# Rotary embedding of q and k without rotation products: 32-row blocks exchanged by ScalarE's copies

## What is computed

```
x1, x2 = xf[..., :half], xf[..., half:]
return jnp.concatenate([x1 * c - x2 * s, x2 * c + x1 * s], axis=-1)
```

## Time and profile before

| | |
|---|---|
| median of 3 runs | 912.7 us (911.99 to 912.81) |
| the profiled execution's own time | 912.49 us |
| its span, first to last instruction | 910.7 us |
| TensorE matmuls busy | 890.3 us, 98% |
| VectorE busy | 604.7 us, 66% |
| ScalarE busy | 454.3 us, 50% |
| GpSimd busy | 44.3 us, 5% |
| granted TensorE clock, mean | 0.998 |

### The profile page before, as it was taken

The page is one execution under the profiler, slowest core; times in us unless marked ns, Lnnn a source line. Parts: engine busy times, 40 slices in busy tenths (PEclk is TensorE's granted clock), DMA queues, the critical chain, the costliest instruction groups (busy, mean ns, idle before and its releaser), DMA issues.

```text
span 910.7 us, 15439 instructions
## 1 busy us (share of the span) xinstructions
PE 890.3 (98%) x6574; PEld 752.5 (83%) x6574; DVE 604.7 (66%) x966; ACT 454.3 (50%) x731; POOL 44.3 (5%) x61
## 2 busy tenths in 40 slices
PE   7999999999899999999999999999999999999997
PEld 5999988787789888888889978776788788888885
DVE  4577978557766666656766477877863566666673
ACT  4775444346443444546544356484622545555561
POOL 0010000010000000000000440000000000000000
PEclk9999999999999999999999999999999999999999
DMA  9544333233578665555339574353817566665521
GB/s 341 186 139 140 97 100 110 72 95 117 206 254 278 185 185 187 189 202 203 108 130 222 137 223 145 127 186 96 276 44 208 141 188 189 192 192 192 200 95 47
DMA packets 131205, 150.78 MB, mean 166 GB/s; under 512 B 11808, under 2 KB 102176, under 8 KB 131008
## 3 DMA queue, kind: packets, MB, share of 16 engines
q1 hardware_dynamic: 129920, 145.57, 51.6%
q10 hardware_dynamic: 1216, 4.23, 1.2%
HBM read 148.73 MB, written 1.05 MB: 164 GB/s over the span
## 4 chain that ended last, share of the span: by engine, by line
PE 90%; DVE 4%; ACT 2%; issue 2%; DMA 1%; POOL 0%; POOLq 0%; ACTq 0%; DVEq 0%
PE psum L834 12%; PE psum L721 10%; PE psum L723 9%; PE psum L722 9%; PE psum L839 7%; PE psum L807 4%; PE psum L808 4%; PE psum L816 4%; PE psum L787 4%; PE psum L727 3%; PE psum L883 2%; PE psum L893 2%; PE psum L884 2%; PE psum L840 2%; PE psum L1724 2%
## 5 line engine op out<-in xcount | busy, mean ns | idle before, releaser
L1827 ACT ACTIVATE parts<-low 128x1024 fp32r<-128x1024 f32 (+3 forms) x252 | 254.3, 1044 | 66.3 <-PE psum L723 50.2
L2710 DVE TENSOR_TENSOR parts<-low,parts 128x1024 fp32r<-128x1024 f32 (+3 forms) x156 | 187.9, 1234 | 27.6 <-ACT parts L1827 27.4
L721 PE MATMUL psum<-parts 128*128 128x512 f32 (+2 forms) x424 | 169.4, 399 | 1.8 <-DVE parts L2710 1.0
L723 PE MATMUL psum<-parts 128*128 128x512 f32 (+2 forms) x424 | 163.5, 386 | 0.0
L722 PE MATMUL psum<-parts 128*128 128x512 f32 (+2 forms) x424 | 163.4, 385 | 0.0
L1827 ACT ACTIVATE high<-psum 128x512 f32<-128x512 f32 (+4 forms) x95 | 52.4, 562 | 162.0 <-PE psum L840 76.4
L834 PE MATMUL psum<-parts 128*128 128x512 f32 x462 | 116.8, 392 | 0.0
L834 PEld LDWEIGHTS psum<-parts 128*128 128x128 f32 x462 | 86.9, 188 | 16.9
L721 PEld LDWEIGHTS psum<-parts 128*128 128x128 f32 x424 | 79.6, 188 | 23.3 <-issue 4.0
L723 PEld LDWEIGHTS psum<-parts 128*128 128x128 f32 x424 | 79.6, 188 | 16.3
L722 PEld LDWEIGHTS psum<-parts 128*128 128x128 f32 x424 | 79.8, 188 | 14.2 <-issue 0.2
(11 more groups left out here) (317 smaller groups left out, 1340.0 us busy)
## 6 DMA issues: line engine op xcount, KB each, us to landing
low<-in_w_in_dram SPq DMA_DIRECT2D x40, 1024.0 KB, 5.3
low<-in_w_ffn_in_dram SPq DMA_DIRECT2D x44, 512.0 KB, 5.2
low<-in_w_ff_in_dram SPq DMA_DIRECT2D x16, 1024.0 KB, 5.9
low<-in_w_ff_out_dram SPq DMA_DIRECT2D x16, 1024.0 KB, 4.9
low<-in_w_ffn_out_dram SPq DMA_DIRECT2D x11, 1024.0 KB, 4.9
low<-in_w_out_dram SPq DMA_DIRECT2D x8, 1024.0 KB, 5.3
low<-in_w_ple_gate_dram SPq DMA_DIRECT2D x4, 1024.0 KB, 4.9
low<-consts_dram ACTq DMA_DIRECT2D x1, 2142.0 KB, 9.0
```

Of the source, the lines that this page charges most:

```text
L721: mm(o, l[0], r[0], start, False)
L723: return mm(o, l[1], r[0], False, stop)
L1827: return e.activation(o, a, ACT.Copy)
L2710: tt(rslot3(n, nk, width)[:, r, 0:w], slot3(n, nk, width)[:, r, 0:w], st.hi3(j)[:, r, 0:w].bitcast(F32), ALU.subtract) \
```

## The change

- The constant rotation matrix goes, and with it `rotate` of TensorE and its 11 products. The table of constants is 128 columns shorter. The table of sines now holds -sin in the first 32 rows of each head and +sin in the other 32.
- ScalarE's `rope_read` makes four copies of 32 rows out of the bank (`swapped`), each to the neighbouring 32-row block, and signals behind the fourth. In block two they go straight to the place of the result (`rope_to`), so the buffers `rz2` go.
- VectorE's sine product takes the exchanged copy in SBUF instead of the product in PSUM, and in block two works in place.
- In block two VectorE makes the cosine product too, from the chunk's bank, at the start of its turn for the next chunk and before the sine product. The bank is freed by this product and no longer by ScalarE's copy. GpSimd keeps the sum. VectorE waits for GpSimd's sum of chunk n - 2 before it writes `rt2` again.
- In block one the cosine product still comes from VectorE, in its old place, and waits as before for ScalarE's signal, which now stands behind the fourth copy.

```diff
-            def rotate(tag, n, m, z):
-
-                b = 2 + n % 2 if tag == "qk" else 5 + n % 3
-                p = bank(b)
-                q.wait_ge(*rope_act.at(tag, n))
-                mm(p[:, 0:256 * m], const(C_ROT, 128), z, True, True).then_inc(rope_pe.up(tag, n), 1)
-                free[b] = [rope_dve.at(tag, n)]
...
             def read2(n):
-                return [main_act.at("qa", n) if n < 2 else rope_act.at("in2", n)]
+                return [main_act.at("qa", n) if n < 2 else rope_dve.at("in2", n, "cos")]
...
+            def swapped(dst, z):
+
+                for p in range(4):
+                    t = copy(dst[32 * p:32 * p + 32], z[32 * (p ^ 1):32 * (p ^ 1) + 32])
+                return t
+
             def rope_read(tag, n, m, b, zs):
-                if n >= (2 if tag == "qk" else 4):
-                    q.wait_ge(*(rope_pe.at(tag, n - 2) if tag == "qk" else rope_pool.at(tag, n - 2)))
-                copy(zs, halves(bank(b))[:, 0:m, :]).then_inc(rope_act.up(tag, n), 1)
+                if tag == "qk" and n >= 2:
+                    q.wait_ge(*rope_dve.at(tag, n - 2))
+                swapped(zs, halves(bank(b))[:, 0:m, :]).then_inc(rope_act.up(tag, n), 1)
...
-            def rotate(tag, n, m, dst, sin):
-                q.wait_ge(*rope_pe.at(tag, n))
-                tt(dst, halves(bank(2 + n % 2 if tag == "qk" else 5 + n % 3))[:, 0:m, :], rep(sin, m), ALU.mult).then_inc(rope_dve.up(tag, n), 1)
+            def rotate(tag, n, m, zs, dst, sin):
+                q.wait_ge(*rope_act.at(tag, n))
+                tt(dst, zs, rep(sin, m), ALU.mult).then_inc(rope_dve.up(tag, n), 1)
...
-            def cosines(n, b):
-                q.wait_ge(*rope_act.at("qk", n))
-                tt(rt1[n % 2], halves(bank(b)), rep(const(C_COS, 256), 2), ALU.mult).then_inc(rope_dve.up("qk", n, "cos"), 1)
+            def cosines(tag, n, m, b, t1, cos):
+                q.wait_ge(*rope_act.at(tag, n))
+                tt(t1, halves(bank(b))[:, 0:m, :], rep(cos, m), ALU.mult).then_inc(rope_dve.up(tag, n, "cos"), 1)
...
             def rotate2(n):
                 if n >= 2:
-                    rotate("in2", n, 1 if n == 6 else 2, rope_to(n), const(C_SINC if n == 6 else C_SIN, 256))
+                    m = 1 if n == 6 else 2
+                    if n >= 4:
+                        q.wait_ge(*rope_pool.at("in2", n - 2))
+                    cosines("in2", n, m, rope_bank[n], rt2[n % 2][:, 0:m, :], const(C_COSC if n == 6 else C_COS, 256))
+                    rotate("in2", n, m, rope_to(n), rope_to(n), const(C_SINC if n == 6 else C_SIN, 256))
...
-            def rope(tag, n, m, zs, t1, cos):
-                q.wait_ge(*rope_act.at(tag, n))
-                tt(t1, zs, rep(cos, m), ALU.mult).then_inc(rope_pool.up(tag, n, "cos"), 1)
-
             def rotate(tag, n, dst, t1):
                 q.wait_ge(*rope_dve.at(tag, n))
-                q.wait_ge(*rope_pool.at(tag, n, "cos"))
                 tt(dst, dst, t1, ALU.add).then_inc(rope_pool.up(tag, n), 1)
```

More of the change, by code:

```diff
@@ L20 @@
 S0 = math.exp(-0.5)
-C_ID, C_SU, C_IU, C_LI, C_ONE, C_BLK, C_ROT, C_M0, C_D64 = [128 * i for i in range(9)]
-C_LV = 128 * 9
+C_ID, C_SU, C_IU, C_LI, C_ONE, C_BLK, C_M0, C_D64 = [128 * i for i in range(8)]
+C_LV = 128 * 8
 C_MA = C_LV + 768
@@ L572, in program @@
         main_pe, main_act, main_dve, main_pool = [count("main_" + n) for n in ("pe", "act", "dve", "pool")]
-        rope_pe, rope_act, rope_dve, rope_pool = [count("rope_" + n) for n in ("pe", "act", "dve", "pool")]
+        rope_act, rope_dve, rope_pool = [count("rope_" + n) for n in ("act", "dve", "pool")]
         rw_pe, rw_act, rw_dve, rw_pool = [count("rwkv_" + n) for n in ("pe", "act", "dve", "pool")]
@@ L1003, in qkv @@
                 for n in range(6):
-                    yield from feature_chunk(st1, QK_AT + n, next(pg), [128, 128], [rope_dve.at("qk", n, "cos")],
-                                             (lambda n=n: rotate("qk", n - 1, 2, rz1[(n - 1) % 2])) if n else nothing)
+                    yield from feature_chunk(st1, QK_AT + n, next(pg), [128, 128], [rope_dve.at("qk", n, "cos")], nothing)
             def gate(r, late):
@@ L1011, in gates @@
                 for r in (2, 3, 0, 1):
-                    yield from gate(r, (lambda: rotate("qk", 5, 2, rz1[1])) if r == 2 else nothing)
+                    yield from gate(r, nothing)
             rw_bank = itertools.cycle((4, 5, 6, 7))
@@ L1457, in tensor_program @@
             st2 = ST["st2"]
[L1459 to L1462, removed]
             def read2(n):
-                return [main_act.at("qa", n) if n < 2 else rope_act.at("in2", n)]
-            turns.beside(head("in2", (0, 2), read2, lambda n: rotate2(n - 1)), seam("in2", 1, True), 3)
+                return [main_act.at("qa", n) if n < 2 else rope_dve.at("in2", n, "cos")]
+            turns.beside(head("in2", (0, 2), read2, nothing), seam("in2", 1, True), 3)
             def main_b():
                 for n in range(2, 7):
-                    yield from feature_chunk(st2, n - 2, next(pg), plan_2[n][1], read2(n), lambda n=n: rotate2(n - 1))
-                yield from token_range(st2, 5, 2, 464, lambda i: [main_act.at("vt2", i), main_dve.at("vt2", i)], lambda: rotate2(6))
+                    yield from feature_chunk(st2, n - 2, next(pg), plan_2[n][1], read2(n), nothing)
+                yield from token_range(st2, 5, 2, 464, lambda i: [main_act.at("vt2", i), main_dve.at("vt2", i)], nothing)
             turns.alone(main_b())
@@ L2831, in qkv @@
                     b = next(pg)
-                    yield from feature_chunk(st1, QK_AT + n, [128, 128], lambda: cosines(n, b), (lambda n=n: rotate1(n - 1)) if n else nothing)
+                    yield from feature_chunk(st1, QK_AT + n, [128, 128], lambda: cosines("qk", n, 2, b, rt1[n % 2], const(C_COS, 256)),
+                                             (lambda n=n: rotate1(n - 1)) if n else nothing)
             def gate(r, late):
@@ L3836, in second2 @@
                     rotate("in2", n, rope_to(n), rt2[n % 2][:, 0:1 if n == 6 else 2, :])
-            turns.beside(head("in2", st2, first2, lambda n: second2(n - 1)), seam("in2", 1, True), 3)
+            turns.beside(head("in2", st2, nothing, lambda n: second2(n - 1)), seam("in2", 1, True), 3)
             def main_b():
                 for n in range(2, 7):
-                    yield from feature_chunk(st2, n - 2, plan_2[n][1], lambda: first2(n), lambda: second2(n - 1))
+                    yield from feature_chunk(st2, n - 2, plan_2[n][1], nothing, lambda: second2(n - 1))
                 yield from token_range(st2, 5, 2, lambda: second2(6))
```

19 lines of the change are left out of this document (6 added, 13 removed).

## The result

The changed kernel takes 915.8 us, median of six executions (914.3 to 916.6), against 912.8 for the kernel before beside it (912.0 to 913.0, six executions): a ratio of 1.0033, 95% interval 1.0023 to 1.0044. The forecast was 914.0 with a range of 909.5 to 916.3, so the range held and the sign was right, but the size was not: +1.3 was forecast, +3.0 came. The outcome that the prediction held likeliest, no change beyond 1.8 us (chance 0.54), did not come; a slower kernel (0.30) did. The profiled execution took 916.38 us with a span of 914.0 (from its first to its last instruction), 3.3 longer than the span before. Its own time is 3.9 longer: in every execution of the kernel before and of e1 some 1.8 to 1.9 us of the time lie outside the span, and in every one of a kernel with block two's change 2.2 to 2.4. So about 0.5 of the +3.0 is lost where no trace looks; why is open.

A forecast was written before the change was run, and what follows sets the result against it. TensorE, busy 98% of the span, bounds the kernel, but new waits outweigh the removed products: +2.47 in block one less 1.13 in block two is +1.34 us, so 914.0 against the median 912.70; range 909.5 to 916.3.

The forecast's parts named there:

- The copies' pitch, 0.60: ScalarE's four copies start 0.60 us apart, so the last ends 1.80 us later than the single copy did.
- A: The start of ScalarE's copy of a chunk out of PSUM, the chunk's end on TensorE; times count from it.
- the overlapping case: ScalarE's four copies go at 0.50 us each, as copies of the same rows do: 912.2 us, chance 0.13.
- the rival in which a change of rows costs more: ScalarE's four copies take longer than 0.60 us each; at 0.72 it gives 916.2 us, chance 0.13.
- Block one, +2.47: Chain's work behind VectorE's longer wait frees TensorE's PSUM banks later: 0.39 + 0.39 + 1.48 + 0.21 = 2.47 us lost.
- Level 1: Block one's chunks 0 and 1: VectorE's queue sets the time and hides the late copy; gain 0.
- Level 4: Block one: four short copies on VectorE free the banks; TensorE's second group at A + 7.83, 1.48 us later.
- Block two's stall, 0.72: TensorE waits 0.72 us, once, for the second half of VectorE's weight split, wanted at A + 6.51, ready at A + 7.23.
- the gain up to chunk 5's end: Block two: three rotations removed bring 2.58 us, less 0.72 waited: 1.86 us.
- The tail, +0.73: Block two's half-size chunk 6: TensorE resumes at A + 6.93 instead of A + 6.20, 0.73 us later.
- the delays stay hidden: Rival: TensorE's products go and no wait takes their place; 912.7 - 9.0 = 903.7 us, chance 0.14.
- The change does what it says: Denies the rival that TensorE keeps waiting for ScalarE or the copies run as one; no chance of its own.

The follow-up runs named there:

- e1: The kernel before with the change in block one alone; 914.77 us, ratio 1.0025 to the kernel before.
- e9b: The changed kernel with e9's tail order, but banks keep their turn and chunk 6's copies and products stand ahead of the second split; 912.80 us.
- a1: The changed kernel, unaltered, run and profiled again; 915.16 us.
- e2: The kernel before with the change in block two alone; 913.09 us, ratio 1.0005, and 913.49 us in a second group of runs.
- e6: The changed kernel with VectorE's cosine product ahead of ScalarE's four copies in block one's chunks 2 to 5; 911.38 us, ratio 0.9984.
- e3: The changed kernel with a single copy of 128 rows for the four, leaving out the exchange of rows; 908.03 us, ratio 0.9951.
- e9: The changed kernel with the tail reordered: value projection's first weights split ahead of chunk 5's copies and products, chunk 6 in a free bank; 917.50 us, ratio 1.0055.
- e10: The changed kernel with two more copies of 32 rows ahead of chunk 5's four; 916.51 us.
- e7: e6 with e9's tail, and with cosine product and splits first in all of block two; 914.52 us, ratio 1.0027.

## Why the prediction was right, and where it was not

- **The copies' pitch, 0.60.** Right: 112.37, 112.97, 113.57 and 114.17, and the cosine product at A + 2.42 for 2.43. The Trainium skill ("ScalarE: Activation LUTs", section "What ACT_TABLE_LOAD costs") states that back-to-back ACTIVATEs overlap by about 93 ns; it gives this for 128 rows and without a condition on rows. It does not hold for these copies: 0.59 long and 0.60 apart, no overlap, while copies of the same rows stand 0.50 apart. It is not for want of another bank: in e9b the next chunk's first copy reads another bank and still starts 0.61 behind the one before (526.05 and 526.66). With an overlap the sum would have been near nothing. So the overlapping case, and the rival in which a change of rows costs more, both fell.
- **Block one, +2.47.** The mechanism was right and the size nearly. Level 1 nothing, as said: TensorE's second group starts 0.34 later (108.11 for 107.77), which is the 0.32 by which VectorE's queue lay later from the start; in a1's profile of the same kernel it starts at 107.72. Levels 2 and 3 brought +0.44 and +0.43 for 0.39, level 5 +0.21 for 0.21. Level 4 brought +1.15 for 1.48: TensorE takes the group at A + 7.82, for 7.83 in the working, but the term subtracted 6.35, the first start of that group in the trace of before, and that group paused for 0.32 within its first products (of line 1217 one starts at 140.83 and the next but one at 141.27, 0.44 later and not 0.12), which the later start swallows. The prediction's working left that pause out. Sum 2.23. TensorE's waits before L1204 on levels 1 to 4 come to 1.4, 1.0, 1.0 and 2.1, together 5.5, for the 6.5 forecast; level 5 has 0.9.
- **Block two's stall, 0.72.** In the profiled execution it was 0.95, and in the other half of the split, and the gain up to chunk 5's end was 1.61 for 1.86. The weights land only at 507.14 there, a term that the prediction did not have, so GpSimd's sum is already under way when VectorE's first half starts. It is this half that TensorE waits for (0.59), then shortly for the second. In a1's execution of the same kernel the weights are there in time and all comes as worked out: VectorE is first, its second half ends at A + 7.10 for 7.18, TensorE takes it at A + 7.15 for 7.23, the stall is 0.73 and the gain 1.82. GpSimd's and VectorE's timelines, the changed kernel first and then a1:

```profile
508.18 1.29 POOL L3696 TENSOR_TENSOR high<-high 128x512 f32<-128x512 f32 x1 [19.02 <-DVE high L2771]
508.25 3.44 DVE L2698 TENSOR_TENSOR parts<-low,parts 128x1024 fp32r<-128x1024 f32 x2 [0.15 <-ACT parts L1809]
```

```profile
507.79 3.46 DVE L2698 TENSOR_TENSOR parts<-low,parts 128x1024 fp32r<-128x1024 f32 x2
507.95 2.22 POOL L3696 TENSOR_TENSOR high<-high 128x512 f32<-128x512 f32 x1 [19.04 <-DVE high L2771]
```

  Whichever starts first runs at its own length and the other is stretched: the sum takes 1.29 where it is first and 2.22 where it is second, and VectorE's two halves take 2.35 with GpSimd idle (109.20). Where the sum is first, VectorE loses what is left of it, less some 0.13: 1.22 left and 1.09 lost here, 1.11 and 0.98 in e2, 0.94 and 0.81 in e9b, 0.50 and 0.37 in e6. The Trainium skill ("SBUF — State Buffer", section "Who interferes with whom") states that a VectorE instruction with two inputs in SBUF contends with a GpSimd instruction that reads SBUF. It also states that the port pair they share is an exclusive lock, and that the order of issue decides who blocks. These traces agree, by the numbers above.
- **The tail, +0.73.** The working of the waits was right: TensorE resumes at A + 6.99 for 6.93, and without the half clock the tail is longer by 0.79 (11.14 against 10.35, in e2 and e6). What was missing is a term: behind a wait of 2.12 and another of 0.54 the clock falls. The prediction gave the tail's wait its length and nothing for what the engine does afterwards. It is 1.57 in the profiled execution (12.71 less 11.14) and 0.99 in a1's.
- **The sum.** In the profiled execution +2.23 - 1.61 + 2.36 = +2.98, and 0.32 from before block one, which is the 3.3 of the span. (Between level 5 and block two a further 0.23 is lost, and won back behind the tail.) Without the clock and the 0.32 it is +1.41 for the forecast +1.34. That it comes so close is in part luck: block one's term was 0.24 too large, and the gain in block two 0.25 too large. The 0.32 is not the change's: a1, the same kernel, has -0.07 at the same place, e1 -0.11 and e3 +0.28, so it differs from one execution to the next. Two terms are missing in the prediction: the half clock, 0.99 to 1.57, and the 0.5 outside the span. By them 914.0 becomes 915.5 to 916.1, for the measured 915.2 and 915.8. That this is still inside the range is luck as well: its upper end, 916.3, was set for copies of 0.72, which did not come.
- **The rivals.** That the delays stay hidden (903.7) fell, as e3 shows: even without any delay the products' 9.0 do not come in, since 4.7 is all that is left of them. The change does what it says.

## What to carry to other kernels

Work taken off the engine that is 98% busy is worth only what the next queue lets through: ask which instruction stands behind the new or longer wait on the engine that receives the work, and how much earlier than its consumer it ends. Here moving one wait in VectorE's queue, with the same work, was worth 3.8 us, more than the whole change. Where a step is moved to take a wait away, the buffers move as well: e9 took away 2.5 us of waits and made one of 2.5 by the order of the banks alone. And a wait of some 2 us on TensorE can cost more than its length, so a sum of waits needs a term for what comes behind each long one.

## What the runs showed of the hardware that I had not expected

- TensorE's granted clock fell from 1.00 to 0.50 (2.4 to 1.2 GHz) behind a wait of 2.1 us or more (3.3 in e10), for 3 to 3.5 us, in five of seven profiles of kernels with the changed tail, and at the end of e7's wait of 2.77 us; e9's 2.50 us was not followed by it. The same matmul took 0.59 instead of 0.37. Price: 0.99 to 1.59 us.
- A copy of 32 rows and 512 columns from PSUM on ScalarE takes 0.59, as long as one of 128 rows (0.60). The exchange costs four times the time for the same data.
- Whichever of GpSimd's sum and VectorE's split (both with two inputs in SBUF) starts first keeps its length, and the other waits for nearly all that is left of it: 2.70 to 3.46 us for the two halves of a split, against 2.35 with GpSimd idle. When the weights land decides which half it is.
- TensorE pauses for 0.3 to 1.5 us inside runs of small products, 2.2 to 2.5 us behind a packet of the queue q8 ("instruction") that comes at the end of a transfer of weights, seven times in five traces; that it waits for instructions is argued.
